# Two chunks of an output projection by Strassen's scheme in a Trainium2 kernel: seven products of half size for eight

## What is computed

```
u = rms_norm(h, norm_gain)                       # h: 512 tokens x 2048
proj = u @ w_in                                  # all attention inputs and gates
y_sb, y_sa = (two attention branches, each gated and projected to 2048)
mixed = sigmoid(g_sb) * y_sb + sigmoid(g_sa) * y_sa      # 512 x 2048
h = h + mixed @ w_out                            # w_out: 2048 x 2048
return rms_norm(h, final_norm_gain)
```

## Time and profile before

| | |
|---|---|
| median of three runs | 1643.45 us (1643.17 to 1644.33) |
| the profiled execution | 1644.75 us |
| its span, first to last instruction | 1643.1 us |
| TensorE busy | 1628.2 us, 99% of the span |
| VectorE busy | 754.4 us, 46% |
| ScalarE busy | 580.9 us, 35% |
| DMA | 101 GB/s over the span |

### The profile page before, as it was taken

The page is one execution under the profiler, slowest core; times in us unless marked ns, Lnnn a source line. Parts: engine busy times, 40 slices in busy tenths (PEclk is TensorE's granted clock), DMA queues, the critical chain, the costliest instruction groups (busy, mean ns, idle before and its releaser), DMA issues.

```text
span 1643.1 us, 20351 instructions
## 1 busy us (share of the span) xinstructions
PE 1628.2 (99%) x7443; PEld 1357.3 (83%) x7443; DVE 754.4 (46%) x1116; ACT 580.9 (35%) x926; POOL 16.2 (1%) x37
## 2 busy tenths in 40 slices
PE   8999999999999999999999999999999999999998
PEld 6888888888888888888888888888888888888886
DVE  5334678622125444354544554444455544434333
ACT  5333333222225454344443233333233433313222
POOL 0000000000000000000000000000000000000000
PEclk9999999999999999999999999999999999999999
DMA  5232233333333322233323333323232523253233
GB/s 195 78 100 79 79 89 90 102 89 91 103 102 91 96 83 83 83 98 88 96 77 103 105 93 96 93 85 95 83 102 83 185 90 103 90 202 121 94 106 115
DMA packets 82043, 165.90 MB, mean 101 GB/s; under 512 B 7104, under 2 KB 7632, under 8 KB 80848
## 3 DMA queue, kind: packets, MB, share of 16 engines
q1 hardware_dynamic: 77808, 150.10, 30.1%
q0 software_dynamic: 3040, 13.63, 2.2%
q10 hardware_dynamic: 1152, 1.57, 0.3%
HBM read 156.90 MB, written 8.39 MB: 101 GB/s over the span
## 4 chain that ended last, share of the span: by engine, by line
PE 98%; DMA 0%; DVE 0%; ACT 0%; issue 0%; SPq 0%; DVEq 0%
PE proj L1098 28%; PE proj L1099 28%; PE proj L1100 28%; PE attn L1099 3%; PE attn L1100 3%; PE attn L1098 3%; PE attn L1259 1%; PE attn L1288 1%; PE attn L1220 1%; PE attn L1219 1%; PE attn L1146 0%; DMA xs<-in_x 0%; PE proj L1166 0%; PE attn L1261 0%; DVE xs L738 0%
## 5 line engine op out<-in xcount | busy, mean ns | idle before, releaser
L1098 PE MATMUL proj<-u_hi,w_hi 128*128 128x512 f32 x1536 | 600.9, 391 | 2.5 <-DVE xs L738 2.5
L1099 PE MATMUL proj<-u_lo,w_hi 128*128 128x512 f32 x1536 | 598.7, 390 | 0.0
L1100 PE MATMUL proj<-u_hi,w_lo 128*128 128x512 f32 x1536 | 598.7, 390 | 0.0
L683 DVE TENSOR_TENSOR w_lo<-stage,w_hi 128x1024 fp32r<-128x1024 f32 x267 | 325.9, 1223 | 518.1 <-ACT w_hi L369 515.5
L369 ACT ACTIVATE w_hi<-stage 128x1024 fp32r<-128x1024 f32 x267 | 282.0, 1060 | 484.6 <-PE proj L1100 356.7
L1098 PEld LDWEIGHTS proj<-u_hi,w_hi 128*128 128x128 f32 x1536 | 288.9, 188 | 61.8 <-DVE xs L738 2.8
L1100 PEld LDWEIGHTS proj<-u_hi,w_lo 128*128 128x128 f32 x1536 | 288.7, 188 | 60.4
L1099 PEld LDWEIGHTS proj<-u_lo,w_hi 128*128 128x128 f32 x1536 | 288.9, 188 | 58.4
L385 ACT ACTIVATE area<-proj 128x512 f32 (+1 forms) x80 | 47.9, 599 | 171.3 <-PE proj L1100 171.2
L1098 PE MATMUL proj<-w_hi,u_hi 128*128 128x512 f32 x256 | 99.9, 390 | 0.0
L1100 PE MATMUL proj<-w_hi,u_lo 128*128 128x512 f32 x256 | 99.6, 389 | 0.0
(11 more groups left out here) (177 smaller groups left out, 1419.9 us busy)
## 6 DMA issues: line engine op xcount, KB each, us to landing
stage<-in_w_in SPq DMA_DIRECT2D x208, 512.0 KB, 3.7
stage<-in_w_out SPq DMA_DIRECT2D x32, 512.0 KB, 3.6
stage<-in_w_branch_sb SPq DMA_DIRECT2D x16, 512.0 KB, 3.6
stage<-in_w_branch_sa SPq DMA_DIRECT2D x16, 512.0 KB, 4.0
xs<-in_x SPq DMA_DIRECT2D x4, 1024.0 KB, 8.7
o_scratch<-og POOLq DMA_DIRECT2D x16, 256.0 KB, 2.3
hres<-in_x POOLq DMA_DIRECT2D x1, 4096.0 KB, 13.6
o_in<-o_scratch POOLq DMA_DIRECT2D x3, 1024.0 KB, 6.1
```

Source lines behind the costliest of these rows:

```text
L683: V.tensor_tensor(w_lo[:, s % RING, :, :], stage[:, s % 2, :, :], w_hi[:, s % RING, :, :].bitcast(F), ALU.subtract).then_inc(strip_lo, 1)
L1098: nc.tensor.matmul(out_, a_hi, b_hi, start=start, stop=False, skip_group_check=free)
L1099: nc.tensor.matmul(out_, a_hi, b_lo, start=False, stop=False, skip_group_check=free)
L1100: return nc.tensor.matmul(out_, a_lo, b_hi, start=False, stop=stop, skip_group_check=free)
```

## The change

Chunks 31 and 32 (columns 512 to 1535 of `w_out`) are computed with Strassen's scheme in the form of Winograd. For each pair of row tiles (a strip, as before) and each chunk, the weights are a 2 by 2 matrix of blocks of 128 rows by 256 columns, and the activations a 2 by 2 matrix of blocks of 128 rows by 256 tokens. Instead of eight products of blocks there are seven: of combined activations with combined weights.

- The activations' combinations `e_raw` (four per pair, E7, E5, E6, E3) are made once and serve both chunks: four VectorE sums per pair (`e_build`, the first of 1024 elements, then 512, 256 and 256), a ScalarE copy to `e_hi` (`e_high`, 1024 elements) and a VectorE difference `e_lo` (`e_low`, 1024). Pairs 0 to 2 are summed in chunk 29, pairs 3 to 5 in chunk 30, pairs 6 and 7 behind it. They stand where `u_hi` and `u_lo` were.
- The weights' combinations, S1 to S4, are made for each of 16 strips (`q` = 0 to 15): SP loads 640 KB in four DMAs of rows of 1 KB (the block (k, 0) twice), VectorE makes three sums (`form_sums`: 512, 256 and 256 elements, each of which needs the one before), ScalarE copies seven blocks to `form_hi` (`form_high`, 1792 elements), and VectorE subtracts (`form_low`, 1792). There are four buffers for the raw and low parts (the low parts overwrite the raw ones) and three for the high ones.
- TensorE does per strip 7 products by 2 token tiles by 3, 42 matmuls of 256 columns, into seven banks of eight (`form_strip`).
- After the eighth strip of a chunk, eleven VectorE sums of 512 elements (`blocks`), each of which needs the one before, add the seven products to the four blocks of `hres`; ScalarE copies the first product to `t_sum`.
- The last chunk's weights are loaded into the places of `e_raw` and `e_hi` (`last_raw`, `last_hi`), from the ninth strip on.
- `hres` holds three chunks' columns now, the fourth's (`hres_last`) is loaded later; `squares` is now `square`, one buffer for its output. The buffers for weights are one ring, in another order in memory.

The core of the diff:

```diff
+    HW = CW // 2
+    FORMS = 7
+    FS = 4 * FORMS * HW
+    RAWS, HIS = 4, 3
+    raw_at = [ring, ring + FS, ring + 4 * FS, ring + 5 * FS]
+    raw = [at(f"raw{r}", [FORMS, HW], F, raw_at[r]) for r in range(RAWS)]
+    form_lo = [at(f"form_lo{r}", [FORMS, HW], R, raw_at[r]) for r in range(RAWS)]
+    form_hi = [at(f"form_hi{r}", [FORMS, HW], R, ring + j * FS) for r, j in enumerate((2, 3, 6))]
...
+            def load_forms(q):
+                if q < 2:
+                    sp.wait_ge(strip_used, NS * C_OUT + 6)
+                elif q < RAWS:
+                    sp.wait_ge(strip_used, NS * C_OUT + NS)
+                else:
+                    sp.wait_ge(form_used, q - RAWS + 1)
+                k, r = 2 * (q % NS), q % RAWS
+                for kt, part, form, copies in ((k, 1, B11, 1), (k + 1, 0, B22, 1), (k + 1, 1, B21, 1), (k, 0, S1, 2)):
+                    sp.dma_start(raw[r][:, form:form + copies, :],
+                                 wout[:, kt:kt + 1, out_cols(q, part)].to_broadcast([P, copies, HW])
+                                 ).then_inc(form_loaded[r], 16)
...
+            def form_high(q):
+                act.wait_ge(form_sum, 3 * q + 3)
+                if q == 0:
+                    act.wait_ge(strip_lo, NS * C_OUT + NS)
+                    act.wait_ge(strip_used, NS * C_OUT + 6)
+                elif q == 1:
+                    act.wait_ge(strip_used, NS * C_OUT + 7)
+                elif q >= HIS:
+                    act.wait_ge(form_used, q - HIS + 1)
+                A(form_hi[q % HIS][:, :, :], raw[q % RAWS][:, :, :], ACT.Copy).then_inc(form_hi_ready, 1)
...
+            for q in range(FAST):
+                form_high(q)
+                if q in (2, 3):
+                    e_high(q + 4)()
+                if q == 3:
+                    for i in range(QT):
+                        act.wait_ge(h_ready, i + 1)
+                        square(0, i)
+                if q == 8:
+                    first_product(0)
+                if q == 11:
+                    act.wait_ge(block_step, BLOCK_STEPS)
+                    for i in range(QT):
+                        square(1, i)
+                if q >= 12:
+                    last_high(q - 12)
...
+            def e_build(p):
+                def f():
+                    if p < 3:
+                        dve.wait_ge(strip_used, NS * (C_OUT - 1) + NS // 2)
+                    else:
+                        dve.wait_ge(strip_used, NS * C_OUT)
+                    dve.wait_ge(mix_lo, 2 * p + 2)
+                    if p:
+                        dve.wait_ge(e_part, 4 * p)
+                    V.tensor_tensor(a_raw[:, :, :].rearrange("p (k h) s -> p k (h s)", k=2),
+                                    area_r[:, 4 * p:4 * p + 3:2, :].bitcast(F),
+                                    area_r[:, 4 * p + 1:4 * p + 4:2, :].bitcast(F), ALU.add).then_inc(e_part, 1)
+                    dve.wait_ge(e_part, 4 * p + 1)
+                    V.tensor_tensor(e_raw[:, p, E7:E5 + 1, :], a_raw[:, 0:2, :], a_raw[:, 1:4:2, :],
+                                    ALU.subtract).then_inc(e_part, 1)
+                    dve.wait_ge(e_part, 4 * p + 2)
+                    V.tensor_tensor(e_raw[:, p, E6, :], e_raw[:, p, E5, :], a_raw[:, 0, :],
+                                    ALU.subtract).then_inc(e_part, 1)
+                    dve.wait_ge(e_part, 4 * p + 3)
+                    V.tensor_tensor(e_raw[:, p, E3, :], a_raw[:, 2, :], e_raw[:, p, E6, :], ALU.add).then_inc(e_part, 1)
+                return f
+            def e_low(p):
+                dve.wait_ge(e_hi_ready, p + 1)
+                V.tensor_tensor(e_lo[:, p, :, :], e_raw[:, p, :, :], e_hi[:, p, :, :].bitcast(F),
+                                ALU.subtract).then_inc(e_lo_ready, 1)
...
+            def form_sums(q):
+                r = q % RAWS
+                dve.wait_ge(form_loaded[r], 64 * (q // RAWS + 1))
+                V.tensor_tensor(raw[r][:, S1:S3 + 1, :], raw[r][:, S1:S3 + 1, :], raw[r][:, B11:B22 + 1, :],
+                                ALU.add).then_inc(form_sum, 1)
+                dve.wait_ge(form_sum, 3 * q + 1)
+                V.tensor_tensor(raw[r][:, S2, :], raw[r][:, S3, :], raw[r][:, B11, :], ALU.add).then_inc(form_sum, 1)
+                dve.wait_ge(form_sum, 3 * q + 2)
+                V.tensor_tensor(raw[r][:, S4, :], raw[r][:, S2, :], raw[r][:, B21, :], ALU.add).then_inc(form_sum, 1)
+            def form_low(q):
+                dve.wait_ge(form_hi_ready, q + 1)
+                V.tensor_tensor(form_lo[q % RAWS][:, :, :], raw[q % RAWS][:, :, :],
+                                form_hi[q % HIS][:, :, :].bitcast(F), ALU.subtract).then_inc(form_lo_ready, 1)
...
+                steps = [(c11, c11, ts, ALU.add, 0), (ts, pr[1], ts, ALU.add, 2), (us, pr[2], ts, ALU.add, 3),
+                         (c11, pr[3], c11, ALU.add, 4), (c21, pr[4], c21, ALU.add, 5), (c12, pr[5], c12, ALU.add, 6),
+                         (c22, pr[5], c22, ALU.add, 0), (c21, c21, us, ALU.add, 0), (c12, c12, ts, ALU.subtract, 0),
+                         (c22, c22, us, ALU.subtract, 0), (c12, pr[6], c12, ALU.add, 7)]
+                for j in range(first, end):
+                    o_, a, b, op, product = steps[j]
+                    if j == 0:
+                        dve.wait_ge(p1_ready, m + 1)
+                    if product == FORMS:
+                        dve.wait_ge(form_used, NS * (m + 1))
+                    elif product:
+                        dve.wait_ge(product_done, (FORMS - 1) * m + product)
+                    if BLOCK_STEPS * m + j:
+                        dve.wait_ge(block_step, BLOCK_STEPS * m + j)
+                    V.tensor_tensor(o_, a, b, op).then_inc(block_step, 1)
...
+            for s in range(LEAD, NS):
+                split_lo(C_OUT, s)
+                if s == 2:
+                    for p in range(3):
+                        e_low(p)
+                if s >= 5:
+                    e_build(s - 2)()
+                if s >= 6:
+                    e_low(s - 3)
+            form_sums(0)
+            e_low(5)
+            form_sums(1)
+            form_low(0)
+            dve.wait_ge(res_loaded, 16)
+            dve.wait_ge(fgain_loaded, 16)
+            for i in range(QT):
+                t = hres[:, i, 0:CW]
+                bank_done(dve, C_OUT, i)
+                V.tensor_tensor(t, proj[i][:, :], t, ALU.add).then_inc(h_ready, 1)
+            for q in range(FAST):
+                if q + 2 < FAST:
+                    form_sums(q + 2)
+                if q + 1 < FAST:
+                    form_low(q + 1)
+                if q in (1, 2):
+                    e_build(q + 5)()
+                if q in (2, 3):
+                    e_low(q + 4)
+                if q == 4:
+                    times_gain(0)
+                if q == 7:
+                    blocks(0, 0, 8)
+                if q == 8:
+                    blocks(0, 8, BLOCK_STEPS)
+                if q == 15:
+                    blocks(1, 0, BLOCK_STEPS)
+                if q >= 12:
+                    last_low(q - 12)
...
+            def product_free(m, p):
+                if m == 0:
+                    if p < 4:
+                        pe.wait_ge(attn_free, 4 * QT)
+                    else:
+                        pe.wait_ge(h_ready, p - 3)
+                elif p == 0:
+                    pe.wait_ge(h_ready, QT)
+                elif p == 1:
+                    pe.wait_ge(p1_ready, 1)
+                else:
+                    pe.wait_ge(block_step, (2, 3, 4, 5, 7)[p - 2])
+            def form_strip(q):
+                m, s = q // NS, q % NS
+                k0, k1 = 4 * s, 4 * s + 2
+                pe.wait_ge(form_lo_ready, q + 1)
+                if m == 0:
+                    pe.wait_ge(e_lo_ready, s + 1)
+                def mixed(slot, half):
+                    def f(t):
+                        cols = slice(P * (2 * half + t), P * (2 * half + t) + P)
+                        return area_r[:, slot, cols], area_r[:, slot + 1, cols]
+                    return f
+                def combined(form):
+                    def f(t):
+                        cols = slice(P * t, P * t + P)
+                        return e_hi[:, s, form, cols], e_lo[:, s, form, cols]
+                    return f
+                products = ((mixed(k0, 0), B11), (combined(E6), S2), (combined(E7), S3), (mixed(k1, 0), B21),
+                            (mixed(k1, 1), S4), (combined(E5), S1), (combined(E3), B22))
+                for p, (left, form) in enumerate(products):
+                    if s == 0:
+                        product_free(m, p)
+                    for t in range(2):
+                        a_hi, a_lo = left(t)
+                        i = mm3(product_bank(m, p)[:, HW * t:HW * t + HW], a_hi, a_lo,
+                                form_hi[q % HIS][:, form, :], form_lo[q % RAWS][:, form, :],
+                                s == 0 and t == 0, s == NS - 1, True)
```

(19 more changed lines are left out.)

218 lines of the change are left out of this document (133 added, 85 removed).

## The result

| | us |
|---|---|
| before, median of 4 runs | 1643.49 (1643.17 to 1644.33) |
| after, median of 4 runs | 1655.08 (1654.68 to 1655.72) |
| ratio, 95% interval | 1.0072, 1.0059 to 1.0085 |
| predicted | 1652.0, range 1646.5 to 1658.5 |

The profiled execution of the changed kernel took 1654.68 us, its span 1653.0. That is 9.9 us over the span of before; the medians lie 11.6 apart. Most of the difference between these two numbers arises ahead of the changed chunks: the profiled execution of before had a fall of the clock at its start, that of after has none there, and so reached chunk 30 1.2 us sooner.

What follows compares the result with a forecast made beforehand. TensorE, busy for 99% of the span, was taken as the bound. Late strips and the clock's fall, 15.0 us, less 6.4 from narrower matmuls, gave 8.6 us slower: 1652.0 from the median 1643.45, range 1646.5 to 1658.5.

Steps and rivals of the forecast that it cites:

- strip 0 late: First strip of chunk 31: its low part comes after VectorE's remaining chunk 30 work; TensorE waits 1.3 us.
- strip 1: Chunk 31: its low part stands behind strip 2's sums, whose loads wait for chunk 30's end; late by 1.7 us.
- strip 3: Chunk 31: its high part on ScalarE stands behind pair 6's, which waits for VectorE's sums; late by 1.0 us.
- strip 4: Chunk 31: its high part on ScalarE stands behind pair 7's copy and four squares; late by 5.9 us, the costliest place.
- strip 9: Chunk 32: its low part on VectorE stands behind eight block sums and strip 10's sums; late by 2.6 us.
- strip 10: Chunk 32: its low part on VectorE stands behind three block sums and strip 11's sums; late by 0.8 us.
- clock: Behind strip 4's idle time TensorE does 3.4 us of work at half speed, 1.7 us lost; ends nothing and 3.4.
- narrower matmuls: Chunks 31 and 32: 256-column matmuls at 0.12 us, 5.04 a strip, 40.3 a chunk against 43.5; 6.4 us less for both.
- T: The prediction's zero of time: the end of chunk 30's last matmul, where the last addition to the residual starts.
- Landing: SP's queue: a strip's four loads land 4.5 us after the first issue, 1.4 of issues plus 3.1; ends 3.7 and 6.1.
- The rival with loads at 6 us: Late loads delay the first strips by 1.5 us more and each from strip 13 on; 4.5 in all, 1656.5 us; chance 0.18.
- The weight loads: Rival: weight loads of 0.19 us hold the narrower matmuls, 672 taking 128 us instead of 87; 1684 us; chance 0.03.

Runs made afterwards that it cites:

- e1: The changed kernel with chunk 30's four squares on ScalarE, and the gain multiplications that need them, moved two strips later; 1651.57 us, ratio 1.0050.
- e2: The changed kernel with activations' sums, high and low parts of pairs 3 to 7 two strips earlier, all in chunk 30; 1648.51 us, ratio 1.0031.
- e3: The changed kernel with unused matmuls of 512 columns in TensorE's idle time, 11 ahead of strip 0 and 21 ahead of strip 4; 1652.73 us, ratio 1.0058.
- e4: e2 without the weights' sums, S1 to S4 being four copies of one quarter, so the output isn't the reference's; 1639.58 us, ratio 0.9975.
- e7: e6 with three DMAs for each strip's weights in place of four; 1644.34 us, ratio 1.0005.
- e6: e5 with seven of chunk 31's block sums, then strip 9's low part and strip 10's sums, then the other four; 1643.58 us, ratio 0.9999.
- e5: e2 with ScalarE's pair copies and VectorE's pair low parts a strip later, strip 1's low part directly behind strip 0's; 1645.68 us, ratio 1.0013.
- e10: e6 with low parts of pairs 6 and 7 behind strip 4's, and the last four block sums two and two around strip 10's; 1641.20 us, ratio 0.9987.

## Why the prediction was right

The time lay 3.1 us above the forecast and inside the range, by the mechanism that it named: 2.3 of the 3.1 in chunks 31 and 32, whose steps follow, the rest in what the medians differ by beyond them. In part it was luck: I had 1.9 us too much for the waits (13.3 for 11.4) and 4.2 too little for what a wait brings with it, the clock and the pauses around it.

| step | forecast | measured |
|---|---|---|
| strip 0 late | 1.3 | 2.8 |
| strip 1 | 1.7 | 0 |
| strip 3 | 1.0 | 0.3 |
| strip 4 | 5.9 | 5.3 |
| strip 9 | 2.6 | 3.0 |
| strip 10 | 0.8 | 0 |
| start to start, 0.26 more for each wait | none | 1.0 |
| clock | 1.7 | 4.9 |
| narrower matmuls | -6.4 | -6.4 |
| sum | 8.6 | 10.9, as read off |

*Strip 4*, the largest term: right in place, chain and size. e1 took the squares out of its chain, and it shrank; e2 took pair 7 out, and it was gone.

*Strip 0* was the mis-sized one among the waits. I let VectorE reach the sums of strip 0 at T - 4.8; they start at 1499.90, and T is 1503.3: T - 3.4. From there to the low part's end my sum gives 6.1 us and the trace 6.2. VectorE's rows (changed kernel):

```profile
1494.84 1.23 DVE L798 TENSOR_TENSOR w_lo<-stage,w_hi 128x1024 fp32r<-128x1024 f32 x1 [0.94 <-ACT w_hi L443]
...
1498.77 1.22 DVE L1172 TENSOR_TENSOR e_lo<-e_raw,e_hi 128x1024 fp32r<-128x1024 f32 x1
1499.90 0.68 DVE L1184 TENSOR_TENSOR raw<-raw 128x512 f32<-128x512 f32 x1
...
1504.08 2.02 DVE L1193 TENSOR_TENSOR form_lo<-raw,form_hi 128x1792 fp32r<-128x1792 f32 x1
```

Three splits start at 1482.68, 1488.76 and 1494.84, 6.1 us apart where TensorE's strips are 5.44: the two engines wait for each other in turn in every strip, ScalarE for the activations' sums and VectorE for the copy. I took those waits as 4 us in all; the trace has 3.87, 2.08 and 0.94 ahead of the splits alone. "I take what lies ahead of T as unchanged" held for TensorE, and hid that the stretch was nearly full.

*Strips 1 and 10* were not late because strips 0 and 9, and the half clock behind each, had put TensorE back by more. Lateness of neighbours doesn't add: what counts is the largest.

*The clock* is the term that failed most. I charged one fall, behind the longest wait. There were three, behind 2.81, 5.28 and 3.00 us of idle time. My own row for it had been a wait of 2.55 us, shorter than what I forecast for strip 9, so it spoke for at least two. e3 shows what they cost in the end: 2.5 us in the profiled execution, for the one behind strip 0 lay within a time that strip 4 would have waited anyway.

*Landing*: I put it at 4.5; strip 9's set was there 5.0 us after strip 5's end. The issues took 1.3 us, as forecast; the 256 KB of the last load took 3.65 us, for which I had 3.1. The medians:

```profile
raw<-in_w_out SPq DMA_DIRECT2D x48, 128.0 KB, 2.7
raw<-in_w_out SPq DMA_DIRECT2D x16, 256.0 KB, 3.6
```

256 KB in rows of 1 KB need the 3.6 us that 512 KB in rows of 2 KB needed. The Trainium skill (DMA: Bandwidth & Descriptors, Specifications) lets rows of 512 bytes and up run at full rate. These medians don't settle it: a time that depends little on the size would explain them, and so would a lower rate for the shorter rows. "At most 4.1" didn't follow from the rule in any case: 1.4 us of issues and up to 3.6 for the load would have allowed 5.0, the measured value. The rival with loads at 6 us and lateness from strip 13 on fell: none of strips 10 to 15 waits in the changed kernel.

*The narrower matmuls* are 0.12 apart as in the earlier trace rows, not 0.109 as by the formula that the Trainium skill (TensorE: Matmul & The Clock Gate, Back-to-back issue gap) gives for the isolated gap. The chain at 1575 (changed kernel):

```profile
1575.98 0.12 PE proj L1317
1576.10 0.12 PE proj L1315
```

In the changed kernel ten strips have neither a wait nor a fall of the clock, and each takes 5.04 us from start to start, to the hundredth what I forecast. Both chunks are 80.6 us of matmuls, and the saving is the 6.4. The weight loads, a rival of 3%, played no part: e4 shows the saving whole once its waits are added back.

## What to carry over

A transformation that saves matmuls pays with elementwise work. Compare it not with idle shares over the kernel but with the queue of each helping engine at the first strip, at every place where a one-off (an activation's sum, a square, a block sum) stands ahead of something TensorE waits for, and against the landing of loads. Here 6.4 us of matmuls could be saved, 17.3 us were lost to order and clock, and moving one-offs into the helpers' own idle time brought 13.9 of them back: from +11.6 to -2.2 us. A wait that you remove shows the next in line, so look at the trace after each.

## What the hardware showed that I had not expected

- The length of a wait alone doesn't say whether the clock falls. It fell behind 2.13 (e7), 2.45 (e6) and 2.56 us (e5), each ahead of strip 0; it didn't behind 2.79 (e3) and 3.02 us (e5), both ahead of strip 9, where it did behind 3.00 (after) and 3.06 (e2). This row is e5 directly behind the latter, at full clock:

```profile
1555.50:1559.50 4.00, 4.00 (x34) 4.00 (x35) 3.79 (x7) 0.45 (x1) 0.00 (x0) 1.00 0.65 187
```

- Waits of 0.3 to 1.6 us in chunks 31 and 32 brought no fall in the profiled executions: some twenty of them in ten kernels.
- A wait costs 0.26 us more than the idle time in brackets. That time counts from the modelled end of the matmul ahead, 0.28 us behind its start, where the next could have started after 0.12: 0.16 more. And the second matmul behind the wait starts 0.22 behind the first, in place of 0.12: 0.10 more (a strip behind a wait takes 5.14 us in place of 5.04). My expectation for e10 has the first part only, and puts it behind the wait. The changed kernel at strip 9:

```profile
1561.00 0.28 PE L1317 MATMUL proj<-form_hi,e_lo 128*128 128x256 f32 x1
1564.28 0.39 PE L1315 MATMUL proj<-form_hi,area_r 128*128 128x256 f32 x1 [3.00 <-DVE form_lo L1193]
1564.50 0.28 PE L1316 MATMUL proj<-form_lo,area_r 128*128 128x256 f32 x1
```

- Open: what decides whether the clock falls behind a wait of 2 to 3 us, and whether e10's last 2.9 us of waits can be hidden. Neither was tried further.
